# Low halves of six weight units per MLP pair: an accumulating transfer in place of a VectorE subtraction

## The chip, the cores and the metric

The kernel runs on one core of a Trainium2 chip. The metric is device time in microseconds, from the start to the end of one execution: the median over runs. The engines that matter here are TensorE (PE, the matmuls), VectorE (DVE), ScalarE (ACT), GpSimd (POOL), SyncE (SP, which only issues transfers) and the 16 DMA engines that move data for the queues of SP and POOL.

## The reference

Two layers of a decoder trunk on 256 tokens with a model width of 2048, all in float32. Each layer has a front part (a wide projection, sparse attention, a convolution branch, cross-attention, gates, an output projection) and then the part that the change touches, the MLP with a hidden width of 8192:

```
h2 = rms_norm(x, norm2_g[l])
x  = x + jnp.square(jax.nn.relu(h2 @ w_up[l])) @ w_down[l]
```

Weights are read from HBM once per layer. No weight stays on the chip.

## The kernel before, in words

**Split products.** PE is given float32 numbers in a rounded form. To keep the accuracy, each operand is written as a high part and a low part, and a product is three matmuls: high by high, high by low, low by high (function `product`, lines 877 to 879, and `unit`, lines 670 to 672). A weight tile is therefore prepared twice before PE may use it: ACT copies the raw tile into the rounded form (`hi`), and DVE subtracts that from the raw tile (`lo = raw - hi`).

**Units and rings.** SP loads weights in chunks of 1 MB (128 partitions by 4 by 512 numbers) into `raw`, which has four slots. One chunk is two *units*, and a unit is 128 by 1024 numbers of `raw`. The split parts lie in `hi` and `lo`, which have four places each, so unit number i of a pair uses place i % 4. ACT may write `hi` of a unit only when PE has finished the unit four before it (`unit_done`), DVE waits for ACT (`hi_ready`), and PE waits for DVE (`lo_ready`). SP loads a chunk into a slot again when the low parts of the units that lay there are made.

**Pairs.** In the MLP two column blocks of 512 are worked on together as a *pair* of 16 units (`seven_products`). For a quarter of the rows the pair saves one product in eight by multiplying sums of tiles. This is why units have different sizes on PE: units 0 and 1 are 6 matmuls each, units 2 and 3 are 12 each, units 4 and 5 only 3 each, units 6 to 11 are 12 each, then 24 matmuls with sums of weights (`w_sum`) follow, and units 12 to 15 are 12 each: 186 matmuls. The rows of the pair's eight chunks go through the slots a, b, c, d, b, d, a, c, where a to d are the four slots of `raw`. So the sixth chunk (units 10 and 11) is loaded into the slot where units 6 and 7 lay.

**Number of pairs.** A layer has four quarters (`qu`) of the hidden width, and a quarter has four pairs `j`: 0 and 1 for `w_up`, 2 and 3 for `w_down`. The last quarter of the first layer has only the first two and uses plain units for the rest. That makes 14 + 16 = 30 pairs. In pairs 1 and 2 of a quarter PE also turns the hidden numbers between its units (16 transposes, line 683), in pairs 0 and 3 it does not.

**Order.** Each engine's program is a list written out by hand. ACT does `hi` of each unit in order, with its other work between (`side_of_pair`, `hidden_of_pair`). DVE does `lo` of each unit in order, with the sums of weights (line 1767), their low parts (line 1771) and sums of results between. POOL has almost nothing to do in the MLP: one load of a gain vector (line 2106).

Of the kernel before, what the change touches and what calls it, by code (L numbers as in the profile page):

```python
# [15 lines left out]


# [1 line left out]

# [1 line left out]

# [3 lines left out]
F32 = mybir.dt.float32  # L25
F32R = mybir.dt.float32r
I32 = mybir.dt.int32
ALU = mybir.AluOpType
# [178 lines left out]
def paired(l, qu):  # L207

    return qu < FFN // D - 1 or l == LAYERS - 1


W_SUMS_AT = [6, 7, 8, 9]
# [63 lines left out]
def build(nc, x, mem, positions, norm1_g, w_in, q_norm_g, k_norm_g, mem_norm_g, w_mem_kv, mq_norm_g,  # L276
# [3 lines left out]
    with ctx:  # L280
# [148 lines left out]
        landed = [sem(f"landed{c}") for c in range(CHUNKS)]  # L429
        hi_ready = sem("hi_ready")  # L430
        lo_ready = sem("lo_ready")
        unit_done = sem("unit_done")
        acc_free = [sem(f"acc_free{i}") for i in range(2)]
        tp_full = sem("tp_full")
# [135 lines left out]
        @block.sync  # L570
        def _(sp):
            here = Place(["unit"])

            def load(c, source):

                sp.wait_ge(lo_ready, here.next("unit", 2))
                sp.sem_inc(waited, 1)
                c = here.ring[c]
                sp.dma_start(raw[:, c, :, 0:source.shape[-1]], source).then_inc(landed[c], 16)

            def load_pair(pair, source, c0):

                units = here.now("unit")
                slots = here.pair_slots()
                for k, (b, c) in enumerate(PAIR_CHUNKS):
                    here.next("unit", 2)
                    if k < 4:
                        sp.wait_ge(lo_ready, here.now("unit"))
                    elif k < 6:
                        sp.wait_ge(lo_ready, units + (12, 16)[k - 4])  # L590
                    else:
                        sp.wait_ge(w_summed, 4 * pair + 4)
                    sp.sem_inc(waited, 1)
                    sp.dma_start(raw[:, slots[k]], source[c, :, :, bass.ds(c0 + b * COL, COL)]).then_inc(landed[slots[k]], 16)

            for l in range(LAYERS):
                for q, (g, c) in enumerate(FRONT_CHUNKS):
                    view, c0, w = FRONT_SRC[g]
                    if l == 0 and q < CB:
                        cols = slice(q * COL, (q + 1) * COL)  # L600
                        if q == 1:
                            sp.wait_ge(first_gain[0], 16)
                            sp.sem_inc(waited, 1)
                        if q > 1:
                            sp.wait_ge(landed[q - 2], 16)
                            sp.sem_inc(waited, 1)
                        sp.dma_start(gain[:, cols], rows(norm1_g[0, cols])).then_inc(first_gain[q], 16)
                        sp.dma_start(x_tok[:, :, cols], x_rows[:, :, cols]).then_inc(x_in[q], 16)
                    if l == 0 and q == 0:
                        sp.wait_ge(lo_ready, here.next("unit", 2))  # L610
                        sp.sem_inc(waited, 1)
                        for half, there in enumerate((landed[0], first_rest)):
                            ks = slice(2 * half, 2 * half + 2)
                            sp.dma_start(raw[:, 0, ks, 0:w], view[l, c, :, ks, c0:c0 + w]).then_inc(there, 16)
                        continue
                    load(q % CHUNKS, view[l, c, :, :, c0:c0 + w])
                for cb in range(CB):
                    for i in range(3):
                        for c in range(CHUNKS):
                            load(c, v_in[l, c, :, :, bass.ds(GATE0 + i * D + cb * COL, COL)])  # L620
                    load(0, v_co[l, 0, :, :, bass.ds(cb * COL, COL)])
                    load(1, v_mo[l, 0, :, :, bass.ds(cb * COL, COL)])
                    load(2, v_ao[l, 0, :, :, bass.ds(cb * COL, COL)])
                    load(3, v_ao[l, 1, :, :, bass.ds(cb * COL, COL)])
                for b in range(CB):
                    for c in range(CHUNKS):
                        load(c, v_out[l, c, :, :, b * COL:(b + 1) * COL])
                for qu in range(FFN // D):
                    for j in range(2):
                        load_pair(pair_number(l, qu, j), v_up[l], qu * D + 2 * j * COL)  # L630
                    if paired(l, qu):
                        for j in range(2):
                            load_pair(pair_number(l, qu, 2 + j), v_down[l, qu], 2 * j * COL)
                        continue
                    for b in range(CB):
# [16 lines left out]
        def _(pe):  # L652
# [3 lines left out]
                pe.sem_inc(s, 1)  # L656
            pe.wait_ge(ready, 1)

            def unit(u, a_hi, a_lo, kts, w, pair, first, last):

                if first:

                    pe.wait_ge(acc_free[pair], here.next(f"acc{pair}"))
                pe.wait_ge(lo_ready, here.next("unit") + 8)
# [44 lines left out]
            def ikw_unit(s, u, first, last):  # L709

                if first:
                    pe.wait_ge(sc_free[0], here.next("sc0"))
                pe.wait_ge(lo_ready, here.next("unit") + 8)
# [175 lines left out]
            def seven_products(l, qu, j):  # L889
# [7 lines left out]
                for i, (b, u) in enumerate(PAIR_UNITS):  # L897
# [14 lines left out]
                    pe.wait_ge(lo_ready, here.next("unit") + 8)  # L912
# [108 lines left out]
        def _(act):  # L1021
# [254 lines left out]
            def split_of_pair(i, slots):  # L1276
# [6 lines left out]
                if b == 1 and u < SEVEN:  # L1283
                    act.activation(hi[:, i % 4, 1], raw[:, c, 2 * (i % 2) + 1], ACT.Copy).then_inc(hi_ready, 1)
                else:
                    act.activation(hi[:, i % 4], raw[:, c, 2 * (i % 2):2 * (i % 2) + 2], ACT.Copy).then_inc(hi_ready, 1)  # L1286

            def side_of_pair(i, pair, number):

# [80 lines left out]
        def _(dve):  # L1370
# [301 lines left out]
            def split_of_pair(i, slots):  # L1672

                b, u = PAIR_UNITS[i]
                c, rows_ = slots[i // 2], slice(2 * (i % 2), 2 * (i % 2) + 2)
                dve.wait_ge(hi_ready, here.next("unit"))
                if b == 1 and u < SEVEN:
                    ins = dve.tensor_tensor(lo[:, i % 4, 1], raw[:, c, 2 * (i % 2) + 1],
                                            hi[:, i % 4, 1].bitcast(F32), ALU.subtract)
# [241 lines left out]
        def _(pool):  # L1921
# [30 lines left out]
            def side(n, l):  # L1952
# [65 lines left out]
                if n == LN_APPLY:  # L2018
# [3 lines left out]
                    pool.tensor_tensor(y_tok[:, :, :], y_tok[:, :, :], over(ln_b[:, :], 1, T),  # L2022
                                       ALU.add).then_inc(ln_scaled, 1)

            def biases(l, c):

                alone()
# [21 lines left out]
            for l in range(LAYERS):  # L2049
# [49 lines left out]
                root(2)  # L2099
                here.next("fill", T * CB + 8 * (FFN // D) + T * (CB - 1))  # L2100

                if l < LAYERS - 1:
                    pool.wait_ge(scaled, here.next("scaled", T + CB))
                    pool.wait_ge(seven_free, pair_number(l, FFN // D - 1, 0))
                    alone()
                    pool.dma_start(gain[:, :], rows(norm1_g[l + 1])).then_inc(gain_in, 16)
                    here.next("scaled", CB - 1)
                here.layer_done()


# [21 lines left out]
```

## Time and profile before

| | |
|---|---|
| time | 2829.12 us, median of 2 runs (2828.1 and 2830.14) |
| profiled execution | span 2827.0 us; no other time of it is recorded, the runs lie 1.1 to 3.1 us above the span |
| PE | busy 2817.1 us, 12924 matmuls and transposes |
| DVE | busy 2063.3 us (73%) |
| ACT | busy 1558.7 us (55%) |
| POOL | busy 185.4 us (7%) |
| DMA | 557.76 MB; SP's queue takes 55.3% of the 16 engines' time, POOL's 3.5% |
| granted PE clock | 1.000 of full speed over the span |

A profile lists the instructions of one execution with their start and length. An engine's idle time is put down to what ended it. A busy PE is a pipelined one: matmuls of 390 ns start every 227 ns, so one lies over the next, and their rate is read from their starts.

### The profile page before, as it was taken

What the parts mean: (1) busy time and instruction counts of PE and PEld (TensorE: products, weight loads), DVE (VectorE), ACT (ScalarE), POOL (GpSimd) and SP (SyncE); (2) the same over time, 40 slices, a digit from 0 to 9 for tenths busy, and PEclk for the clock granted to TensorE, in tenths of its full rate; (3) what the DMA queues carried; (4) which work ended last, traced back from release to release, by engine and by line L of the source; (5) the groups of instructions that cost most, each with busy time, mean ns of one, the idle gap of its engine ahead of it and who ended that gap; (6) DMA issues with size and microseconds to landing.
All of it is one profiled execution on the core that took longest, in us unless ns stands there. A gap on an engine that the chain in (4) does not pass through costs nothing.

```text
span 2827.0 us, 32980 instructions
## 1 busy us (share of the span) xinstructions
PE 2817.1 (100%) x12924; PEld 2332.6 (83%) x12924; DVE 2063.3 (73%) x2247; ACT 1558.7 (55%) x2048; POOL 185.4 (7%) x205
## 2 busy tenths in 40 slices
PE   9999999999999999999999999999999999999999
PEld 7888888888888888888888888888888888888887
DVE  6688656556788888887656976555667887887887
ACT  6777644444554655555448776444455555455463
POOL 1124100000000000000002251000000000000000
PEclk9999999999999999999999999999999999999999
DMA  8655566755565565666566555667555655655645
GB/s 304 210 170 176 167 194 208 238 190 198 178 208 172 202 218 167 210 220 208 180 218 210 169 179 166 194 206 238 194 194 166 220 192 181 215 167 208 214 164 179
DMA packets 274795, 557.76 MB, mean 197 GB/s; under 512 B 13232, under 2 KB 13232, under 8 KB 272464
## 3 DMA queue, kind: packets, MB, share of 16 engines
q1 hardware_dynamic: 268896, 526.68, 55.3%
q0 software_dynamic: 5744, 28.97, 3.5%
q8 instruction: 102, 1.67, 0.2%
q14 instruction: 53, 0.43, 0.0%
HBM read 549.32 MB, written 6.29 MB: 197 GB/s over the span
## 4 chain that ended last, share of the span: by engine, by line
PE 99%; DMA 0%; ACT 0%; DVE 0%; issue 0%; SPq 0%; ACTq 0%; DVEq 0%
PE acc L670 17%; PE acc L672 17%; PE acc L671 16%; PE acc L879 13%; PE acc L878 13%; PE acc L877 13%; PE tp L683 3%; PE sc L879 1%; PE sc L878 1%; PE sc L877 1%; PE tp L878 1%; PE tp L877 1%; PE tp L879 1%; PE sc L733 0%; PE tp L763 0%; PE sc L730 0%
## 5 line engine op out<-in xcount | busy, mean ns | idle before, releaser
L1392 DVE TENSOR_TENSOR lo<-raw,hi 128x1024 fp32r<-128x1024 f32 (+1 forms) x528 | 648.5, 1232 | 491.2 <-ACT hi L1036 485.3
L1036 ACT ACTIVATE hi<-raw 128x1024 fp32r<-128x1024 f32 (+1 forms) x528 | 546.6, 1037 | 611.3 <-PE acc L672 588.4
L1286 ACT ACTIVATE hi<-raw 128x1024 fp32r<-128x1024 f32 x420 | 437.9, 1056 | 556.7 <-PE acc L879 359.7
L1681 DVE TENSOR_TENSOR lo<-raw,hi 128x1024 fp32r<-128x1024 f32 x420 | 509.7, 1221 | 107.1 <-ACT hi L1286 106.3
L670 PE MATMUL acc<-hi,hT 128*128 128x512 f32 x1280 | 509.4, 398 | 1.7 <-DVE lo L1392 1.7
L672 PE MATMUL acc<-hi,hT 128*128 128x512 f32 x1280 | 499.8, 390 | 0.0
L671 PE MATMUL acc<-lo,hT 128*128 128x512 f32 x1280 | 498.6, 390 | 0.0
L877 PE MATMUL acc<-hi,hT 128*128 128x512 f32 x800 | 312.2, 390 | 0.0
L879 PE MATMUL acc<-hi,hT 128*128 128x512 f32 x800 | 311.5, 389 | 0.0
L878 PE MATMUL acc<-lo,hT 128*128 128x512 f32 x800 | 311.4, 389 | 0.0
L672 PEld LDWEIGHTS acc<-hi,hT 128*128 128x128 f32 x1280 | 240.2, 188 | 51.7
L670 PEld LDWEIGHTS acc<-hi,hT 128*128 128x128 f32 x1280 | 240.5, 188 | 49.6 <-issue 2.1
L671 PEld LDWEIGHTS acc<-lo,hT 128*128 128x128 f32 x1280 | 240.8, 188 | 47.2
L877 PE MATMUL acc<-hi,bT_hi 128*128 128x512 f32 x700 | 273.0, 390 | 0.0
L879 PE MATMUL acc<-hi,bT_lo 128*128 128x512 f32 x700 | 272.5, 389 | 0.0
L878 PE MATMUL acc<-lo,bT_hi 128*128 128x512 f32 x700 | 272.4, 389 | 0.0
L670 PE MATMUL acc<-hi,bT_hi 128*128 128x512 f32 x512 | 203.7, 398 | 0.0
L672 PE MATMUL acc<-hi,bT_lo 128*128 128x512 f32 x512 | 199.9, 390 | 0.0
L671 PE MATMUL acc<-lo,bT_hi 128*128 128x512 f32 x512 | 199.5, 390 | 0.0
L877 PEld LDWEIGHTS acc<-hi,hT 128*128 128x128 f32 x800 | 150.2, 188 | 31.4
L879 PEld LDWEIGHTS acc<-hi,hT 128*128 128x128 f32 x800 | 150.2, 188 | 31.3
L878 PEld LDWEIGHTS acc<-lo,hT 128*128 128x128 f32 x800 | 150.2, 188 | 30.8
(331 smaller groups left out, 3951.0 us busy)
## 6 DMA issues: line engine op xcount, KB each, us to landing
raw<-in_w_in SPq DMA_DIRECT2D x159, 1024.0 KB, 5.0
raw<-in_w_up SPq DMA_DIRECT2D x128, 1024.0 KB, 6.0
raw<-in_w_down SPq DMA_DIRECT2D x128, 1024.0 KB, 5.5
raw<-in_w_out SPq DMA_DIRECT2D x32, 1024.0 KB, 5.2
raw<-in_w_mem_kv SPq DMA_DIRECT2D x16, 1024.0 KB, 5.1
raw<-in_w_attn_o SPq DMA_DIRECT2D x16, 1024.0 KB, 5.2
raw<-in_w_conv_o SPq DMA_DIRECT2D x8, 1024.0 KB, 5.1
raw<-in_w_mem_o SPq DMA_DIRECT2D x8, 1024.0 KB, 5.2
```

Source lines behind the costliest of these rows:

```text
L670: pe.matmul(o, a1, w1, start=first and dk == 0, stop=False)
L671: pe.matmul(o, a1, w2, start=False, stop=False)
L672: mm = pe.matmul(o, a2, w1, start=False, stop=last and dk == 1)
L683: mm = pe.transpose(tp[0:m, b, i, 0:k], tile, ident[0:k, 0:k])
L877: pe.matmul(o, a_hi, w_hi, start=first, stop=False)
L878: pe.matmul(o, a_hi, w_lo, start=False, stop=False)
L879: return pe.matmul(o, a_lo, w_hi, start=False, stop=last)
L1036: act.activation(hi[:, u % 4, :, 0:w], raw[:, c, 2 * (u % 2):2 * (u % 2) + 2, 0:w], ACT.Copy).then_inc(hi_ready, 1)
L1286: act.activation(hi[:, i % 4], raw[:, c, 2 * (i % 2):2 * (i % 2) + 2], ACT.Copy).then_inc(hi_ready, 1)
L1392: dve.tensor_tensor(lo[:, u % 4, :, 0:w], raw[:, here.ring[u // 2], 2 * (u % 2):2 * (u % 2) + 2, 0:w], hi[:, u % 4, :, 0:w].bitcast(F32), ...
L1681: ins = dve.tensor_tensor(lo[:, i % 4], raw[:, c, rows_], hi[:, i % 4].bitcast(F32), ALU.subtract)
```

## The change

In every pair, units 6, 7, 9, 12, 13 and 14 no longer get their low part from DVE. ACT writes the high part as before, waits for its own write, and then writes the negated high part into `lo`. POOL waits for that and issues a transfer from `raw` to `lo` that adds what it moves to what lies there, so `lo` ends as `raw - hi`. PE waits for that transfer (`lo_added`, one semaphore for each of the four places) where it waited for DVE. SP waits for it too before it overwrites the raw slot. All other units keep DVE's subtraction. The load of the gain vector stands on POOL between the transfers of the third and the fourth quarter. The diff, cut to its core:

```diff
+DMA_LOW = (6, 7, 9, 12, 13, 14)
+def by_dma(l, qu, j, i):
+    return (j < 2 or paired(l, qu)) and i in DMA_LOW
...
+            def units_split(n):
+                if n > 0:
+                    sp.wait_ge(lo_ready, 8 + LOWS[n])
+                    sp.sem_inc(waited, 1)
+                for r in {m % 4 for m in range(max(n - 8, 0), n) if BY_DMA[m]}:
+                    sp.wait_ge(lo_added[r], 16 * LOWS_MADE[r][n])
+                    sp.sem_inc(waited, 1)
...
                     if k < 4:
-                        sp.wait_ge(lo_ready, here.now("unit"))
+                        units_split(here.now("unit") - 8)
                     elif k < 6:
-                        sp.wait_ge(lo_ready, units + (12, 16)[k - 4])
+                        units_split(units + (4, 8)[k - 4])
...
+            def split_here():
+                n = here.next("unit")
+                if BY_DMA[n - 1]:
+                    pe.wait_ge(lo_added[(n - 1) % 4], 16 * LOWS_MADE[(n - 1) % 4][n])
+                else:
+                    pe.wait_ge(lo_ready, 8 + LOWS[n])
...
                     act.activation(hi[:, i % 4], raw[:, c, 2 * (i % 2):2 * (i % 2) + 2], ACT.Copy).then_inc(hi_ready, 1)
+                    if i in DMA_LOW:
+                        act.wait_ge(hi_ready, here.now("unit"))
+                        act.activation(lo[:, i % 4], hi[:, i % 4].bitcast(F32), ACT.Copy, scale=-1.0).then_inc(minus_hi, 1)
...
-                dve.wait_ge(hi_ready, here.next("unit"))
+                here.next("unit")
+                if i in DMA_LOW:
+                    return
+                dve.wait_ge(hi_ready, here.now("unit"))
...
+            def low_parts(pair):
+                slots = here.pair_slots()
+                for k, i in enumerate(DMA_LOW):
+                    pool.wait_ge(minus_hi, len(DMA_LOW) * pair + k + 1)
+                    alone()
+                    pool.dma_start(lo[:, i % 4].bitcast(F32), raw[:, slots[i // 2], 2 * (i % 2):2 * (i % 2) + 2],
+                                   accum_op=ALU.add).then_inc(lo_added[i % 4], 16)
```

ACT's list in the fourth pair of the program (first layer, first quarter, j = 3), units 4 to 10: the number behind `landed` is the slot of `raw`, and `hi_50`, `lo_51`, `raw_49` are the three buffers. Before:

```order
L1284 ACTIVATE hi_50<-raw_49 128x512 [waits unit_done,landed3]
L1284 ACTIVATE hi_50<-raw_49 128x512 [waits unit_done]
L1286 ACTIVATE hi_50<-raw_49 128x1024 [waits unit_done,landed1]
L1286 ACTIVATE hi_50<-raw_49 128x1024 [waits unit_done]
L1286 ACTIVATE hi_50<-raw_49 128x1024 [waits unit_done,landed0]
```

and in the changed kernel, where line 1286 is line 1324:

```order
L1322 ACTIVATE hi_50<-raw_49 128x512 [waits unit_done,landed3]
L1322 ACTIVATE hi_50<-raw_49 128x512 [waits unit_done]
L1324 ACTIVATE hi_50<-raw_49 128x1024 [waits unit_done,landed1]
L1327 ACTIVATE lo_51<-hi_50 128x1024 [waits hi_ready]
L1324 ACTIVATE hi_50<-raw_49 128x1024 [waits unit_done]
L1327 ACTIVATE lo_51<-hi_50 128x1024 [waits hi_ready]
L1324 ACTIVATE hi_50<-raw_49 128x1024 [waits unit_done,landed0]
```

The negated copies of units 6 and 7 stand directly behind their high parts, ahead of the high part of the next unit.

SP's list around the first pairs. Before (the last loads of the output projection, the first pair's first six and last two chunks, and the third pair's):

```order
L579 DMA raw_49<-in_w_out 128x4x512 [waits lo_ready] x16
L594 DMA raw_49<-in_w_up 128x4x512 [waits lo_ready] x6
L594 DMA raw_49<-in_w_up 128x4x512 [waits w_summed] x2
...
L594 DMA raw_49<-in_w_down 128x4x512 [waits lo_ready] x6
L594 DMA raw_49<-in_w_down 128x4x512 [waits w_summed] x2
```

and in the changed kernel the first pair's first five, its sixth, its last two, and the second pair's first two and third:

```order
L625 DMA raw_49<-in_w_up 128x4x512 [waits lo_ready] x5
L625 DMA raw_49<-in_w_up 128x4x512 [waits lo_ready,lo_added2,lo_added3]
L625 DMA raw_49<-in_w_up 128x4x512 [waits w_summed] x2
L625 DMA raw_49<-in_w_up 128x4x512 [waits lo_ready,lo_added1,lo_added2,lo_added3] x2
L625 DMA raw_49<-in_w_up 128x4x512 [waits lo_ready,lo_added0,lo_added1,lo_added2,lo_added3]
```

The sixth load (units 10 and 11) now waits for the transfers of units 6 and 7. SP's queue is in order, so the loads behind it wait as well.

## Rows read from the trace of the kernel before

**Rows 1.** The page: span, and busy time, share and instructions by engine.

```profile
span 2827.0 us, 32980 instructions
PE 2817.1 (100%) x12924; PEld 2332.6 (83%) x12924; DVE 2063.3 (73%) x2247; ACT 1558.7 (55%) x2048; POOL 185.4 (7%) x205
```

**Rows 2.** All waits of PE: waited for: us in total, times, longest us.

```profile
PE sc L981 <- POOL ident L2038: 3.0, 1, 3.0
PE acc L670 <- DVE lo L1392: 1.7, 1, 1.7
PE tp L683 <- DVE xg L1421: 0.9, 1, 0.9
PE tp L683 <- ACT y_tok L1043: 0.8, 2, 0.4
```

**Rows 3.** The page: splitting groups of the pairs, count, busy us, mean ns, idle.

```profile
L1286 ACT ACTIVATE hi<-raw 128x1024 fp32r<-128x1024 f32 x420 | 437.9, 1056 | 556.7 <-PE acc L879 359.7
L1681 DVE TENSOR_TENSOR lo<-raw,hi 128x1024 fp32r<-128x1024 f32 x420 | 509.7, 1221 | 107.1 <-ACT hi L1286 106.3
```

**Rows 4.** Timeline, fourth pair: PE, last matmul of units 2 and 3, first of unit 6.

```profile
861.96 0.39 PE L879 MATMUL acc<-hi,bT_lo 128*128 128x512 f32 x1
...
864.68 0.39 PE L879 MATMUL acc<-hi,bT_lo 128*128 128x512 f32 x1
...
866.27 0.39 PE L877 MATMUL acc<-hi,bT_hi 128*128 128x512 f32 x1
```

**Rows 5.** Timeline, the same pair: ACT, units 6, 7 to 9, 10, 11, 12 to 13.

```profile
862.45 1.06 ACT L1286 ACTIVATE hi<-raw 128x1024 fp32r<-128x1024 f32 x1 [2.15 <-PE acc L879]
865.11 2.96 ACT L1286 ACTIVATE hi<-raw 128x1024 fp32r<-128x1024 f32 x3 [1.60 <-PE acc L879]
872.80 1.06 ACT L1286 ACTIVATE hi<-raw 128x1024 fp32r<-128x1024 f32 x1 [4.73 <-DMA raw<-in_w_down]
...
875.66 2.94 ACT L1295 ACTIVATE w_sum_hi<-w_sum 128x1024 fp32r<-128x1024 f32 x3
878.51 1.99 ACT L1286 ACTIVATE hi<-raw 128x1024 fp32r<-128x1024 f32 x2
```

**Rows 6.** Timeline, the same pair: DVE, low parts of units 6 and 7.

```profile
863.54 1.23 DVE L1681 TENSOR_TENSOR lo<-raw,hi 128x1024 fp32r<-128x1024 f32 x1 [0.62 <-ACT hi L1286]
...
866.21 1.23 DVE L1681 TENSOR_TENSOR lo<-raw,hi 128x1024 fp32r<-128x1024 f32 x1 [0.30 <-ACT hi L1286]
```

**Rows 7.** Timeline, a pair with transposes (second of a quarter): ACT, unit 6.

```profile
947.91 1.06 ACT L1286 ACTIVATE hi<-raw 128x1024 fp32r<-128x1024 f32 x1
```

**Rows 8.** Timeline, the same pair: PE, first matmul of unit 6.

```profile
952.44 0.39 PE L877 MATMUL acc<-hi,hT 128*128 128x512 f32 x1
```

**Rows 9.** DMA issues of POOL one by one: count, KB, us from issue to landing.

```profile
ln_g<-in_conv_ln_g POOLq DMA_DIRECT2D x1, 256.0 KB, 3.3
x_park<-x_tok POOLq DMA_DIRECT2D x1, 1024.0 KB, 4.3
gain<-in_norm_g POOLq DMA_DIRECT2D x1, 1024.0 KB, 6.8
conv_bias<-in_conv_o_b POOLq DMA_DIRECT2D x1, 256.0 KB, 9.4
```

**Rows 10.** Windows of the fourth pair: us, busy by engine, PE clock, DMA share, GB/s.

```profile
863.00:866.00 3.00, 3.00 (x15) 2.50 (x14) 2.36 (x2) 1.40 (x2) 0.00 (x0) 1.00 0.37 141
866.00:869.00 3.00, 3.00 (x15) 2.45 (x15) 2.79 (x3) 2.07 (x3) 0.00 (x0) 1.00 0.22 17
878.00:881.00 3.00, 3.00 (x14) 2.46 (x14) 3.00 (x4) 2.50 (x3) 0.00 (x0) 1.00 1.05 395
```

**Rows 11.** The page: DMA queue of SP, packets, MB, share of 16 engines.

```profile
q1 hardware_dynamic: 268896, 526.68, 55.3%
```

**Rows 12.** Window of one whole pair's length, columns as in rows 10.

```profile
780.00:824.00 44.00, 44.00 (x203) 36.46 (x203) 36.85 (x39) 26.70 (x31) 0.00 (x0) 1.00 0.56 191
```

More of the change, by code:

```diff
@@ L18 @@
 from contextlib import ExitStack
+from itertools import accumulate
 import numpy as np
@@ L209, in paired @@
     return qu < FFN // D - 1 or l == LAYERS - 1
+DMA_LOW = (6, 7, 9, 12, 13, 14)
+PAIRS = LAST_PAIR + 1
+def by_dma(l, qu, j, i):
+    return (j < 2 or paired(l, qu)) and i in DMA_LOW
+MLP_UNITS = [(l, qu, j, i) for l in range(LAYERS) for qu in range(FFN // D) for j in range(4) for i in range(16)]
+MLP_FIRST = [(l + 1) * GROUPS * UNITS - 2 * UNITS * 4 * (FFN // D) for l in range(LAYERS)]
+BY_DMA = [False] * (LAYERS * GROUPS * UNITS)
+for l_, qu_, j_, i_ in MLP_UNITS:
+    BY_DMA[MLP_FIRST[l_] + 16 * (4 * qu_ + j_) + i_] = by_dma(l_, qu_, j_, i_)
+LOWS = [0, *accumulate(1 - by for by in BY_DMA)]
+LOWS_MADE = [[0] * (LAYERS * GROUPS * UNITS + 1) for r in range(4)]
+for r_ in range(4):
+    LOWS_MADE[r_] = [0, *accumulate(int(by and n % 4 == r_) for n, by in enumerate(BY_DMA))]
 W_SUMS_AT = [6, 7, 8, 9]
@@ L431, in build @@
         lo_ready = sem("lo_ready")
+        minus_hi = sem("minus_hi")
+        lo_added = [sem(f"lo_added{r}") for r in range(4)]
         unit_done = sem("unit_done")
@@ L572, in _ @@
             here = Place(["unit"])
+            def units_split(n):
[5 more added lines that the diff above has]
+                    sp.sem_inc(waited, 1)
             def load(c, source):
-                sp.wait_ge(lo_ready, here.next("unit", 2))
-                sp.sem_inc(waited, 1)
+                units_split(here.next("unit", 2) - 8)
                 c = here.ring[c]
@@ L587, in load_pair @@
                     if k < 4:
-                        sp.wait_ge(lo_ready, here.now("unit"))
+                        units_split(here.now("unit") - 8)
                     elif k < 6:
-                        sp.wait_ge(lo_ready, units + (12, 16)[k - 4])
+                        units_split(units + (4, 8)[k - 4])
                     else:
                         sp.wait_ge(w_summed, 4 * pair + 4)
-                    sp.sem_inc(waited, 1)
+                        sp.sem_inc(waited, 1)
                     sp.dma_start(raw[:, slots[k]], source[c, :, :, bass.ds(c0 + b * COL, COL)]).then_inc(landed[slots[k]], 16)
@@ L609, in _ @@
                     if l == 0 and q == 0:
-                        sp.wait_ge(lo_ready, here.next("unit", 2))
-                        sp.sem_inc(waited, 1)
+                        units_split(here.next("unit", 2) - 8)
                         for half, there in enumerate((landed[0], first_rest)):
@@ L663, in unit @@
                     pe.wait_ge(acc_free[pair], here.next(f"acc{pair}"))
-                pe.wait_ge(lo_ready, here.next("unit") + 8)
+                split_here()
                 for dk, kt in enumerate(kts):
@@ L712, in ikw_unit @@
                     pe.wait_ge(sc_free[0], here.next("sc0"))
-                pe.wait_ge(lo_ready, here.next("unit") + 8)
+                split_here()
                 for dk in range(2):
@@ L911, in seven_products @@
                         hidden_here(u, qu)
-                    pe.wait_ge(lo_ready, here.next("unit") + 8)
+                    split_here()
                     w = [(hi[:, i % 4, dk], lo[:, i % 4, dk]) for dk in range(2)]
@@ L2023, in side, with next_gain @@
                                        ALU.add).then_inc(ln_scaled, 1)
+            def next_gain(l):
+                pool.wait_ge(scaled, here.next("scaled", T + CB))
+                pool.wait_ge(seven_free, pair_number(l, FFN // D - 1, 0))
+                alone()
+                pool.dma_start(gain[:, :], rows(norm1_g[l + 1])).then_inc(gain_in, 16)
+                here.next("scaled", CB - 1)
+            def low_parts(pair):
+                slots = here.pair_slots()
+                for k, i in enumerate(DMA_LOW):
+                    pool.wait_ge(minus_hi, len(DMA_LOW) * pair + k + 1)
+                    alone()
+                    pool.dma_start(lo[:, i % 4].bitcast(F32), raw[:, slots[i // 2], 2 * (i % 2):2 * (i % 2) + 2],
+                                   accum_op=ALU.add).then_inc(lo_added[i % 4], 16)
             def biases(l, c):
@@ L2100, in _ @@
                 here.next("fill", T * CB + 8 * (FFN // D) + T * (CB - 1))
[L2102 to L2107, printed above, removed]
+                for qu in range(FFN // D):
+                    for j in range(4 if paired(l, qu) else 2):
+                        low_parts(pair_number(l, qu, j))
+                    if l < LAYERS - 1 and qu == FFN // D - 2:
+                        next_gain(l)
                 here.layer_done()
```

## The prediction

> **What bounds the kernel now.** I read the page's busy times first: PE is busy for 2817.1 of 2827.0 us [rows 1]. So all idle time of PE is 9.9 us, 0.35% of the span, and no change that leaves PE's matmuls alone can give back more. The view of waits says who causes it: PE waited 6.4 us in all, 5.6 of them in the first microseconds, and not once for a low part in the MLP [rows 2]. VectorE, which the change relieves, is busy for 73%, but nobody on PE's path waits for it. The granted clock is 1.00 in every window I looked at [rows 10, 12]. Last I read the timeline around units 6 and 7 of a pair, because there the distance between "place free" and "PE needs it" is shortest: only units 4 and 5, three matmuls each, lie between.
>
> **What goes away.** 6 x 30 = 180 subtractions at 1.22 us [rows 3]: 220 us of VectorE time. It was hidden under PE and is worth nothing on the path. At most the 9.9 us above could come back, and as the waits of PE lie outside the MLP, I count 0.
>
> **What is added on ScalarE.** 180 negated copies at 1.06 us (the rate of the other copies of that size [rows 3]): 190 us, 6.3 us a pair, where ScalarE is busy 26.7 of 44 us [rows 12]. Throughput is no question, but each stands in a chain, below.
>
> **Units 6 and 7: a new wait of PE.** In the fourth pair PE's last matmul of unit 2 ends at 861.96 + 0.39 = 862.35 and ScalarE starts the high part of unit 6 at 862.45 [rows 4, 5], a handover of 0.10 us. It ends at 863.51. VectorE began at 863.54, ended at 864.77 [rows 6], and PE needed unit 6 at 866.27 [rows 4]: 1.50 us were left over. In the new chain the negated copy runs from 863.54 to 864.60, POOL is told at about 864.70, the transfer takes T from issue to landing, and PE is told 0.10 later. PE is late by 864.80 + T - 866.27 = **T - 1.47 us**. In a pair with transposes the high part starts at 947.91 and PE needs unit 6 at 952.44 [rows 7, 8]: 947.91 + 1.06 + 0.03 + 1.06 + 0.20 + T - 952.44 = **T - 2.18 us**. There are 15 pairs of each kind (j = 0 and 3, j = 1 and 2), so the mean is T - 1.82.
>
> Nothing hides this. ScalarE cannot start sooner, because place 2 of `hi` is free only when unit 2 is done, and when PE stalls the next pair shifts with it, with the same distances. So 30 stalls add up.
>
> **How large is T?** No row shows an accumulating transfer. It moves 512 KB, but reads both the raw tile and the place it adds to, 1 MB in all. POOL's transfers took 3.3 us for 256 KB, 4.3 us for 1 MB that comes from the chip's own memory, and 6.8 us for 1 MB in the middle of the MLP [rows 9]. I take T = 4.3 us: it is the row nearest in source and in bytes read, and the DMA engines are little used in the moment when unit 6 needs them (0.37 and 0.22 of their time [rows 10]). The bounds are 3.3 (fewer bytes than this transfer writes) and 6.8 us. With 4.3 the stalls are 2.83 and 2.12 us, mean 2.48, times 30 = **74 us**. With 3.3 it is 44 us, with 6.8 it is 149 us.
>
> The Trainium skill, "DMA: Bandwidth & Descriptors", section "Anatomy of one DMA", gives 2.0 us and bytes by 436 GB/s for a transfer of this queue: 3.2 us for 512 KB. "Collectives: The Full Stack", section "The bandwidth ceiling", says that an add in a transfer costs no cycles but needs two source reads, which halves the rate: 2.0 + 2.4 = 4.4 us, an estimate from the two pages. By the first the stalls would be 41 us, by the second 77 us; both speak against this change, and no trace of before shows which is right.
>
> Unit 7 brings no second stall. Its high part runs 865.11 to 866.17 [rows 5], the negated copy to 867.26, so the transfer lands at 867.46 + T. PE wants it 12 matmuls or 2.72 us after it began unit 6 late: 866.27 + T - 1.47 + 2.72 = 867.52 + T. That is level, whatever T is.
>
> **Units 10 and 11 come later.** Their load waited for VectorE's low part of unit 7, done at 867.44 [rows 6]; the high part of unit 10 started at 872.80 [rows 5], 5.36 us later. Now the load waits for the transfer: high part at 867.46 + T + 5.36, low part ready 2.3 us later, at 875.1 + T. PE needs it 4 x 2.72 us behind unit 6, at 875.7 + T. This just fits, so I count 0, up to 1 us a pair if the transfer of unit 9 slows that load.
>
> **Units 12 to 14.** Between the start of high part 10 and that of high part 12 ScalarE has 878.51 - 872.80 = 5.7 us of work [rows 5]. So high part 12 starts at about 878.6 + T, its negated copy is done 2.2 us later, and with both handovers the low part lands at 880.9 + T plus its own time T'. PE needs unit 12 after six units and 24 matmuls, 21.8 us behind unit 6: at 886.6 + T. So PE waits if T' is over 5.7 us (by the same steps 6.0 with transposes). Here the loads behind the sixth run back to back and the DMA engines are full, 1.05 of their time [rows 10]. I therefore take the row from the busy middle of the MLP, 6.8 us [rows 9]: 1.1 and 0.8 us, mean 0.9, times 30 = **28 us**. Bounds: nothing with T' under 5.7, and 3.5 x 30 = 105 us with the 9.4 us of a transfer that queued behind another [rows 9].
>
> **Other queues.** SP waits for one to four semaphores more per load; it idles between loads. POOL's gain load stands behind 72 transfers of the first three quarters, and was waiting until then for the same pair anyway; 0. DMA engines: SP's 526.68 MB took 55.3% of 2827 us [rows 11], 2.97 us per MB. Six transfers of 0.52 MB written and 1.05 MB read add 9 to 19 us to a pair of 44 us at share 0.56 [rows 12]: 0.78 to 0.98. The DMA engines do not become the bound by bytes, but little is left.
>
> **Sum.** 74 + 28 = 102 us on the profiled execution, 2827.0 to 2929. The median of the runs is 2.1 us above the profiled span, so 2931 us, 3.6% slower.
>
> **Rivals.**
> 1. *The transfer is short* (T up to about 3.5 us and T' under 5.7). For it: SBUF on both sides, an idle DMA moment. 1 MB took 4.3 us, and at 2.97 us per MB the half of it would need some 1.5 us less, 2.8. Then the stall is 0.6 to 1.3 us, 29 us in all; with T = 3.5 it is 50. The time is 2858 to 2880, not slower by 2%. The point that decides: a mean stall of 1.9 us, T = 3.7. Chance 0.20.
> 2. *Transfers queue on each other and on the loads.* T = 6.8 and the full 105 us at units 12 to 14: 149 + 105, 3083 us. For it: the share near 0.98. Against it: units 6 and 7 fall into a pause of the loads. Something between my sum and this, 2990 to 3083: chance 0.13.
> 3. *PE's clock falls in the stalls.* No row shows it: the longest stall of PE in before was 3.0 us at the start [rows 2], and the clock stood at 1.00 in all windows here. Matmuls start every 227 ns at the upper level (from 864.68 to 866.27 there are seven steps, the last matmul of unit 3 and the six of units 4 and 5 [rows 4]); at the lower of the two levels, 1.2 instead of 2.4 GHz, a unit would take 2.72 us more. If one unit per pair ran so, that is 82 us on top, 3013 us. "TensorE: Matmul & The Clock Gate" of the Trainium skill (Part 1) says that idleness does this. Chance 0.12.
> 4. *VectorE's relief pays.* It would have to shorten PE's own work; the cap is 9.9 us, 2819 us. Faster by 2% is out of reach. Chance of that much 0.01, against.
>
> My forecast, stalls of 1.9 to 5 us a pair at full clock, has 0.54. Two per cent, about what a measurement of this kernel can tell from no change, is 57 us or 1.9 us a pair. So: faster 0.01, same 0.20, slower 0.79. The range reaches from T = 3.1 without the tail (2829 + 38) to a case between rivals 2 and 3 with the sum, 3050: 2867 to 3050. The forecast alone would be 2886 to 2980.
>
> **What would show it.** In the profile of the changed kernel: PE's waits in the MLP name the transfer into `lo`, 30 of them of 2 to 3 us at unit 6, and shorter ones at unit 12; POOL's transfers land 4 to 5 us after issue in the first third of a pair and 6 to 7 us in the last; the DMA share of a pair is 0.7 or more; VectorE's busy time is 220 us lower and ScalarE's 190 us higher. I am wrong if T is under 3.5 us, if PE's waits lie at units 10 to 15 rather than at 6, or if the clock is below 1.00.

## The result, and the profile after

The changed kernel takes 3015.28 us (median of two runs, 3012.7 and 3017.87), the kernel before 2829.12: 1.0659 times as long, with a 95% interval of 1.0639 to 1.0680. The forecast was 2931; the time lies inside the range of 2867 to 3050, 84 us above the forecast and outside the 2886 to 2980 of the forecast at full clock.

The profiled execution is 3010.9 us long, 183.9 us more than [rows 1]. The page of the changed kernel, span and busy times (as [rows 1]), queues ([rows 11]), two splitting groups and the POOL issues ([rows 3]), and the landing time of the new transfers:

```profile
span 3010.9 us, 33864 instructions
PE 2880.2 (96%) x12924; PEld 2359.0 (78%) x12924; DVE 1861.2 (62%) x2067; ACT 1743.1 (58%) x2228; POOL 337.8 (11%) x385
...
q1 hardware_dynamic: 268896, 526.68, 51.3%
q0 software_dynamic: 31664, 123.35, 20.4%
...
L1324 ACT ACTIVATE hi<-raw 128x1024 fp32r<-128x1024 f32 x420 | 440.7, 1053 | 555.9 <-PE acc L917 278.2
L1725 DVE TENSOR_TENSOR lo<-raw,hi 128x1024 fp32r<-128x1024 f32 x240 | 293.5, 1223 | 370.3 <-ACT hi L1324 370.2
...
L2083 POOL DMA_DIRECT2D lo<-raw x180 | 152.2, 846 | 1279.1 <-ACT lo L1327 1211.5
...
lo<-raw POOLq DMA_DIRECT2D x180, 512.0 KB, 5.4
```

VectorE lost its 180 subtractions (202 us) and ScalarE got 184 us. PE does the same 12924 matmuls, but is busy for 63.1 us more and idle for 120.8 us more. These two numbers are the 183.9 us. The waits of PE (us in total, times, longest) account for the idle part. The first two of these lines are new, the third stood in [rows 2] too:

```profile
PE acc L915 <- DMA lo<-raw: 109.0, 44, 4.4
PE acc L915 <- DVE lo L1725: 11.2, 10, 2.0
PE sc L1019 <- POOL ident L2099: 3.0, 1, 3.0
```

The longer busy time is mostly clock. The mean granted clock of the execution is 0.983, and 0.017 x 3010.9 = 51 us (an estimate; some 2 us of it fall into time in which PE stood still anyway). The fourth pair, which [rows 4 to 6] show of before, shows how it comes about. The timeline of ACT (start, duration, what ended the idle time before):

```profile
881.62 1.06 ACT L1324 ACTIVATE hi<-raw 128x1024 fp32r<-128x1024 f32 x1 [2.15 <-PE acc L917]
882.72 1.07 ACT L1327 ACTIVATE lo<-hi 128x1024 fp32r<-128x1024 f32 x1
...
897.96 1.06 ACT L1324 ACTIVATE hi<-raw 128x1024 fp32r<-128x1024 f32 x1 [8.55 <-DMA raw<-in_w_down]
```

and POOL's issue for unit 6:

```profile
884.36 0.85 POOL L2083 DMA_DIRECT2D lo<-raw  x1 [20.66 <-ACT lo L1327]
```

and PE, from the last matmul of unit 5 on:

```profile
885.22 0.39 PE L917 MATMUL acc<-hi,hidT_sum_lo 128*128 128x512 f32 x1
889.16 0.79 PE L915 MATMUL acc<-hi,bT_hi 128*128 128x512 f32 x1 [3.55 <-DMA lo<-raw]
889.75 0.63 PE L916 MATMUL acc<-lo,bT_hi 128*128 128x512 f32 x1
890.18 0.63 PE L917 MATMUL acc<-hi,bT_lo 128*128 128x512 f32 x1
890.60 0.63 PE L915 MATMUL acc<-hi,bT_hi 128*128 128x512 f32 x1
```

The negated copy ends at 883.79. POOL starts to issue 0.57 us later, the transfer lands 4.8 us after that, and at 889.16 PE goes on, after 3.55 us without work. Then its matmuls start every 427 ns instead of the 227 ns of [rows 4]: the lower of the two clock levels, 1.2 instead of 2.4 GHz. The windows over the same stretch (columns as in [rows 10]) say the same in the clock column:

```profile
884.00:888.00 4.00, 1.61 (x8) 0.99 (x6) 1.08 (x2) 3.68 (x4) 1.69 (x2) 1.00 0.61 115
888.00:892.00 4.00, 2.84 (x7) 2.27 (x8) 3.66 (x4) 1.38 (x2) 0.85 (x1) 0.55 0.96 182
892.00:896.00 4.00, 4.00 (x13) 3.12 (x12) 0.00 (x0) 0.00 (x0) 0.00 (x0) 0.60 1.02 236
896.00:900.00 4.00, 4.00 (x19) 3.31 (x18) 0.94 (x1) 2.04 (x3) 0.00 (x0) 1.00 1.05 398
```

The column to be careful with is PE's busy time: at 892 to 896 it is 4.00 of 4.00 us, and yet only 13 matmuls ran, where 896 to 900 holds 19. The last two columns show the other surprise: the DMA engines are at 0.96 of their time while they move 182 GB/s; with loads alone a full share is some 400.

Each stall of PE can be put to the unit that it stands before, by its time and by the transfer that lands in that moment. Against the terms of the prediction:

| where the 183.9 us are | predicted | measured |
|---|---|---|
| unit 6, 30 stalls: 3.2 to 3.4 us in most pairs without transposes, 2.4 to 2.6 in most others | 74 | 91.2 |
| units 9 and 10: 7 stalls on a transfer, 10 on VectorE | 0 | 24.7 |
| units 12 to 14, 7 stalls | 28 | 4.3 |
| clock below 1.00 | 0 | 51 |
| PE busy longer, clock aside (63.1 - 51; the last section has a reading) | 0 | 12 |
| other idle time of PE | 0 | 0.6 |

### The profile page after: what moved, and what is told of

It is laid out like the page before. It is cut to its first block, busy times and chain, and to the rows that moved or that the text cites. A ratio compares the mean times of both kernels' runs of the same rounds, so it can differ in the third digit from the quotient of the medians.

```text
span 3010.9 us, 33864 instructions
## 1 busy us (share of the span) xinstructions
PE 2880.2 (96%) x12924; PEld 2359.0 (78%) x12924; DVE 1861.2 (62%) x2067; ACT 1743.1 (58%) x2228; POOL 337.8 (11%) x385
## 4 chain that ended last, share of the span: by engine, by line
PE 81%; DMA 11%; ACT 5%; issue 1%; DVE 1%; POOL 0%; SPq 0%; POOLq 0%; ACTq 0%; DVEq 0%
PE acc L708 16%; PE acc L710 16%; PE acc L709 15%; PE acc L915 9%; PE acc L916 9%; PE acc L917 9%; DMA lo<-raw 7%; PE tp L721 2%; ACT hi L1324 2%; DMA raw<-in_w_up 2%; DMA raw<-in_w_down 2%; ACT lo L1327 1%; ACT w_sum_hi L1336 1%; PE sc L917 1%; PE sc L916 1%
## 5 line engine op out<-in xcount | busy, mean ns | idle before, releaser
L1725 DVE TENSOR_TENSOR lo<-raw,hi 128x1024 fp32r<-128x1024 f32 x240 | 293.5, 1223 | 370.3 <-ACT hi L1324 370.2
L708 PE MATMUL acc<-hi,hT 128*128 128x512 f32 x1280 | 509.4, 398 | 2.4 <-DVE lo L1433 2.4
L710 PE MATMUL acc<-hi,hT 128*128 128x512 f32 x1280 | 499.8, 390 | 0.0
L709 PE MATMUL acc<-lo,hT 128*128 128x512 f32 x1280 | 498.6, 390 | 0.0
L915 PE MATMUL acc<-hi,hT 128*128 128x512 f32 x800 | 327.0, 409 | 70.0 <-DMA lo<-raw 64.0
L915 PE MATMUL acc<-hi,bT_hi 128*128 128x512 f32 x700 | 284.8, 407 | 50.4 <-DMA lo<-raw 45.1
L916 PE MATMUL acc<-lo,hT 128*128 128x512 f32 x800 | 322.3, 403 | 0.0
L917 PE MATMUL acc<-hi,hT 128*128 128x512 f32 x800 | 321.3, 402 | 0.0
L2083 POOL DMA_DIRECT2D lo<-raw x180 | 152.2, 846 | 1279.1 <-ACT lo L1327 1211.5
L916 PE MATMUL acc<-lo,bT_hi 128*128 128x512 f32 x700 | 280.7, 401 | 0.0
L710 PEld LDWEIGHTS acc<-hi,hT 128*128 128x128 f32 x1280 | 240.2, 188 | 51.6
L917 PE MATMUL acc<-hi,bT_lo 128*128 128x512 f32 x700 | 280.4, 401 | 0.0
L708 PEld LDWEIGHTS acc<-hi,hT 128*128 128x128 f32 x1280 | 240.5, 188 | 50.6 <-issue 2.6
L709 PEld LDWEIGHTS acc<-lo,hT 128*128 128x128 f32 x1280 | 240.7, 188 | 47.2
L915 PEld LDWEIGHTS acc<-hi,hT 128*128 128x128 f32 x800 | 156.2, 195 | 117.2 <-DMA lo<-raw 75.8
L915 PEld LDWEIGHTS acc<-hi,bT_hi 128*128 128x128 f32 x700 | 136.2, 195 | 90.9 <-DMA lo<-raw 33.2
L708 PE MATMUL acc<-hi,bT_hi 128*128 128x512 f32 x512 | 203.7, 398 | 0.0
L710 PE MATMUL acc<-hi,bT_lo 128*128 128x512 f32 x512 | 199.9, 390 | 0.0
L709 PE MATMUL acc<-lo,bT_hi 128*128 128x512 f32 x512 | 199.5, 390 | 0.0
```

What stands on the lines that cost most here:

```text
L915: pe.matmul(o, a_hi, w_hi, start=first, stop=False)
L916: pe.matmul(o, a_hi, w_lo, start=False, stop=False)
L917: return pe.matmul(o, a_lo, w_hi, start=False, stop=last)
L1725: ins = dve.tensor_tensor(lo[:, i % 4], raw[:, c, rows_], hi[:, i % 4].bitcast(F32), ALU.subtract)
L2083: pool.dma_start(lo[:, i % 4].bitcast(F32), raw[:, slots[i // 2], 2 * (i % 2):2 * (i % 2) + 2], accum_op=ALU.add).then_inc(lo_added[i % 4] ...
```

## The experiments

My theory was that of the prediction: a transfer costs where the distance from "high part written" to "PE needs it" is shorter than the chain, which is at unit 6 above all. The rival: the transfers and the loads slow each other, wherever they meet. Two questions stood beside that: what makes one transfer so long, and whether the lost clock comes from the stalls or from the transfers as such.

### No low parts at all: what VectorE's relief is worth

The six units get no low part from anyone; PE and the loads wait for the high part only.

```diff
-                    pe.wait_ge(lo_added[(n - 1) % 4], 16 * LOWS_MADE[(n - 1) % 4][n])
+                    pe.wait_ge(hi_ready, n)
```

> The low parts of the six units are not made at all, neither by VectorE nor by a transfer: PE uses what lies in the place, and waits for the high part alone. It shows what taking the six subtractions off VectorE is worth when nothing replaces them. If VectorE is off PE's path, as the waits of before say: 2824 to 2829 us, no more than the 9.9 us in which PE idled. If VectorE's load slows PE in a way that the waits do not show: under 2800 us.

Measured: 2828.94 us, 1.0001 [0.9991, 1.0010]. Taking 180 subtractions out of VectorE without putting anything in their place gives nothing back, within 0.1%. So nothing that replaces them can win time through VectorE's relief.

### Which units cost

Only the list of units changes, as here; the others are the same line with (7, 9, 12, 13, 14), (9, 12, 13, 14), (12, 13, 14) and (12,):

```diff
-DMA_LOW = (6, 7, 9, 12, 13, 14)
+DMA_LOW = (6, 7)
```

> Only units 6 and 7 by a transfer. Slack theory: the 30 stalls at unit 6 (91 us in the changed kernel) and the time that the lower clock takes behind them (some 60 us) stay, the stalls at units 9 and 12 to 14 (some 15 us) go: 2975 to 2995 us. Rival, load on the DMA engines: one third of the transfers, so about one third of 186 us: 2890 us.

> Unit 6 is back on VectorE, 7, 9, 12, 13, 14 stay with the transfer. Slack theory: place 3 is free when unit 3 is done, and PE needs it three units later; the chain for unit 7 is as long as that for unit 6, so the stall moves from unit 6 to unit 7 and keeps its size, about 3.4 us in pairs 0 and 3 and 2.4 us in pairs 1 and 2: 2990 to 3015 us. If the stall were due to two transfers in a row or to unit 6 alone, it goes: 2860 to 2900 us.

> Units 6 and 7 are back on VectorE, 9, 12, 13 and 14 stay with the transfer. Slack theory: no stall at 6 or 7; at unit 9 the high part ends at 868.1 in the fourth pair of before, the chain at about 874.7 with a landing of 5.0, PE needs it at 874.4: 0.3 us; in pairs with transposes ScalarE is 1 to 2 us later: about 2 us. 15 x 0.3 + 15 x 2 = 35 us and a little by the clock: 2850 to 2885 us. Rival, load on the DMA engines: four of six transfers, some 2950 us.

> Only units 12, 13 and 14 of each pair get their low part by a transfer; 6, 7 and 9 are back on VectorE. Slack theory (a transfer costs PE what the chain of high part, negated copy, hand-over and transfer takes beyond the time between 'place free' and 'PE needs it'): units 12 to 14 have about 13 us from place free to use, the chain takes 8 to 10 us, so no stall at units 6 to 10, full clock, and 2829 to 2840 us. Rival, the transfers cost by loading the DMA engines and queueing with the weight loads: the DMA engines are at a share of 1.0 just where these three run, so three of six transfers keep about half of the 186 us: some 2920 us.

> Unit 12 alone by transfer. With units 12 to 14 its transfer took 8.3 us (median) to land and TensorE waited 2.1 us in each pair. If it is the two transfers issued 2 and 4 us behind it that slow it, it lands in 5.0 to 6.5 us now, no wait is left, and the time is 2829 to 2840. Rival: the loads of weights slow it by themselves: 7.5 us or more, waits of 1 to 2 us in each pair, 2860 to 2900.

Measured (the cost of the clock is one minus the mean granted clock, times the span):

| units by transfer | us | ratio to before | PE waits on a transfer | clock |
|---|---|---|---|---|
| 6, 7, 9, 12, 13, 14 | 3015.3 | 1.0659 [1.0639, 1.0680] | 109.0 in 44 | 51 |
| 7, 9, 12, 13, 14 | 3020.0 | 1.0674 [1.0652, 1.0695] | 106.3 in 44 | 54 |
| 6, 7 | 2971.9 | 1.0506 [1.0485, 1.0527] | 90.1 in 31 | 50 |
| 9, 12, 13, 14 | 2886.2 | 1.0201 [1.0184, 1.0218] | 38.9 in 52 | 0 |
| 12, 13, 14 | 2916.2 | 1.0301 [1.0284, 1.0318] | 63.4 in 30 | 32 |
| 12 | 2920.6 | 1.0325 [1.0304, 1.0346] | 60.3 in 29 | 26 |

(Waits and clock are those of the profiled execution. With 12, 13 and 14 it was 2926.8 us long, the longest of that kernel's runs, 2909.1 to 2926.8.)

Units 6 and 7 behaved as the distances said: the second to the fourth row of the table lie only 5 us above, 3 below and 1 above their expected ranges. Taking unit 6 out saves nothing, because unit 7 then stalls PE in its place (84.8 us in 30 stalls). What fell are my expectations for the late units. I had expected hardly a wait with 12 to 14 alone, and the number came out at the rival's 2920. The run with unit 12 alone settles why: there too the rival was right, and its 2860 to 2900 us were even 20 us short, because the waits were 2.1 us each and the clock fell. One transfer alone, with no other behind it, still lands late. From its page, the transfers' count, size and landing time:

```profile
lo<-raw POOLq DMA_DIRECT2D x30, 512.0 KB, 8.1
```

One pair of it in windows of 2 us:

```profile
892.00:894.00 2.00, 2.00 (x11) 1.65 (x10) 1.17 (x2) 2.00 (x4) 0.85 (x1) 1.00 1.06 387
894.00:896.00 2.00, 2.00 (x11) 1.65 (x10) 2.00 (x3) 1.43 (x2) 0.00 (x0) 1.00 1.03 368
896.00:898.00 2.00, 2.00 (x11) 1.65 (x10) 0.10 (x1) 0.00 (x0) 0.00 (x0) 1.00 1.08 310
898.00:900.00 2.00, 1.51 (x7) 0.93 (x5) 0.37 (x1) 0.00 (x0) 0.00 (x0) 1.00 0.84 170
```

POOL's timeline there:

```profile
892.67 0.85 POOL L2083 DMA_DIRECT2D lo<-raw  x1 [45.10 <-ACT lo L1327]
```

and PE's, first matmul of unit 12:

```profile
900.73 0.50 PE L915 MATMUL acc<-hi,bT_hi 128*128 128x512 f32 x1 [1.22 <-DMA lo<-raw]
```

At issue the loads keep the DMA engines full (1.06), and for the first 4 us nearly all bytes are theirs. The transfer lands 8.0 us after issue, and PE starts. It does not take its siblings to slow it.

In the changed kernel the same transfer meets fewer loads. What the queues moved in the 4 us behind its issue in the fourth pair (packets, MB, share of 16 engines), first with unit 12 alone, from 892.67:

```profile
q1 hardware_dynamic: 734, 1.47, 102.2%
```

and then in the changed kernel, from 906.38:

```profile
q0 software_dynamic: 126, 0.52, 65.2%
q1 hardware_dynamic: 323, 0.63, 42.8%
```

With unit 12 alone POOL's queue (q0) moved nothing in these 4 us. In the changed kernel the loads (q1) moved 0.63 MB beside it, and the transfer landed in 4.8 us. SP's timeline says why fewer loads are left there: the sixth, seventh and eighth load of that pair (start of the first, us to the end of the third issue), before, with units 12, 13 and 14 alone, and in the changed kernel:

```profile
867.52 6.59 SPq L594 DMA_DIRECT2D raw<-in_w_down  x3
879.20 6.60 SPq L625 DMA_DIRECT2D raw<-in_w_down  x3
891.85 2.54 SPq L625 DMA_DIRECT2D raw<-in_w_down  x3
```

The seventh and the eighth wait for VectorE's sums of weights (`w_summed`). In the changed kernel the sixth is held until unit 7's transfer has landed, the sums are made by then, and the other two go out with it.

The table's other lesson is that rows do not add up. Unit 12 alone costs more than units 12, 13 and 14 together with 9. A stall gives everything behind it a lead: the loads, ScalarE and the transfers go on while PE stands. With unit 9 in the list, PE waits some 0.7 us there and reaches unit 10 1.1 us later (counted from its start of unit 8, means of 30 pairs); unit 12's transfer goes out 0.4 us sooner. Together that is the 1.5 us by which the wait at unit 12 fell, from 60.3 to 16.0 us, 2.0 to 0.5 a pair. The 0.4 us are probably not the lead: VectorE no longer makes unit 9's low part and ends its sums of weights 1.1 us sooner. No run separates the two. And waits of 1.6 us at most, 52 of them, left the granted clock at 1.00, where 31 waits of mostly 2.4 to 3.4 us cost 50 us of clock.

### What makes the transfer long

First without the add (the low part is then the raw weight), then with the add for the first half of the unit only (the second half stays the negated high part):

```diff
-                    pool.dma_start(lo[:, i % 4].bitcast(F32), raw[:, slots[i // 2], 2 * (i % 2):2 * (i % 2) + 2],
-                                   accum_op=ALU.add).then_inc(lo_added[i % 4], 16)
+                    pool.dma_start(lo[:, i % 4].bitcast(F32), raw[:, slots[i // 2], 2 * (i % 2):2 * (i % 2) + 2]
+                                   ).then_inc(lo_added[i % 4], 16)
```

```diff
+                    pool.dma_start(lo[:, i % 4, 0].bitcast(F32), raw[:, slots[i // 2], 2 * (i % 2)],
+                                   accum_op=ALU.add).then_inc(lo_added[i % 4], 16)
```

> The six transfers move the raw weights without adding (so the low part is wrong: it is the raw weight); all waits stay. It prices the addition. If the addition costs by its second read: the DMA time of one transfer falls from 2.9 us of all 16 engines to about 1.5, its landing in the quiet moment of unit 6 from 4.5 to about 3.1 us, the stalls at unit 6 from 3.3 and 2.6 to about 1.9 and 1.2 us, 46 us in all, and with less or no fall of the clock 2880 to 2910 us. If a transfer of POOL's queue costs the same with and without the addition: 3015 us.

> The six transfers add only the first half of the unit (128 by 512), the second half keeps the negated high part (a wrong low part). It splits the landing of 4.5 us into a fixed part and one by bytes. If the bytes set it (2.9 us of DMA time for the whole): 3.1 us, the stalls at unit 6 about 1.9 and 1.2 us, 2880 to 2910 us. If the fixed part sets it: landing over 4 us, 2990 to 3015 us.

Measured: 2966.59 us, 1.0485 [1.0464, 1.0506], and 2983.79 us, 1.0546 [1.0525, 1.0567]. Neither range was hit. The transfers themselves did what the first theory said. Landed one by one, the transfer of unit 6 takes 4.5 us (median of 30) in the changed kernel, 3.3 with half of it added and 2.8 as a plain copy. The time of the DMA engines comes from the queue's share on each page. The kernel without low parts gives the base of that queue:

```profile
q0 software_dynamic: 5744, 28.97, 3.4%
```

The page of the kernel with plain copies:

```profile
span 2963.9 us, 33864 instructions
...
q0 software_dynamic: 31664, 123.35, 11.5%
```

Plain: (0.115 x 2963.9 - 0.034 x 2826.4) / 180 = 1.36 us of all 16 engines for one transfer. With the add: (0.204 x 3010.9 - 96) / 180 = 2.88 us. The same bytes by the page's count take 2.1 times as long. "Collectives: The Full Stack" of the Trainium skill, section "The bandwidth ceiling", says of the add in a ReduceScatter that it needs two source reads, which halves the rate. The factor of 2.1 here agrees with that; that the second read is the reason here too is not shown.

But the gain did not reach the end. The waits of PE with plain copies:

```profile
PE acc L915 <- DMA lo<-raw: 97.1, 57, 4.1
```

At unit 6 the stalls fell from 91.2 to 38.9 us, the amount that 4.5 to 2.8 us gives (30 x 1.7 = 51). At unit 9 they rose from 13.5 us in 7 stalls to 54.7 us in 25, and unit 9's transfer took 7.0 us (median) to land instead of 5.6, although it now takes half of the DMA engines' time. SP's next loads, which wait for units 6 and 7, are released sooner and run into unit 9's transfer: in the fourth pair the first of them goes out 0.09 us before it (881.06 and 881.15), in the changed kernel 1.86 us behind it (891.85 and 889.99). And with shorter stalls PE gives less lead. With half of the unit added it is the same: 46.6 us at unit 6 and 52.1 at unit 9. A faster transfer moved the wait by three units.

### Is it the stall that lowers the clock, and does a stall give a lead?

Matmuls into an unused accumulator stand ahead of PE's wait at unit 6, as long as the stalls there: 15 in pairs j = 0 and 3, 11 in j = 1 and 2, but none in the first pair of a layer.

```diff
+                    if i == 6 and not first_of_layer:
+                        for _ in range(15 if j in (0, 3) else 11):
+                            pe.matmul(sc[:, 1], hT_hi[:, 0, 0:P], hT_hi[:, 0:2], start=True, stop=True)
```

First with all six units:

> The changed kernel, and PE does matmuls of 128 by 512 that nobody reads (15 in pairs 0 and 3 of a quarter, 11 in pairs 1 and 2, none in the first pair of a layer) between unit 5 and its wait for unit 6: 366 matmuls of 227 ns, 83 us, about as long as the stalls. If the lower clock is a consequence of PE standing idle at unit 6: the stalls turn into work, the clock stays at 1.00, and the 60 us go: about 2955 us although PE does more. If the clock falls for another reason, or the lost time is not the clock: 3010 to 3020 us, as the changed kernel. If the stalls were not where I put them, the matmuls come on top: 3095 us.

Measured: 3028.52 us, 1.0704 [1.0688, 1.0720]. The 2955 us did not come. The clock rose from 0.983 to 0.992, and the stalls at unit 6 fell to 0.7 us or less, except in the two pairs that have no fill. But at unit 9 the seven long ones grew from 0.9 to 2.6 us to 2.4 to 3.9, and waits on VectorE's low parts grew from 11.2 us in 10 to 23.4 in 19. The lead would explain it: those seven lie in pairs j = 1, where PE in the changed kernel loses some 2.6 us at unit 6 and 1.7 us by the clock behind it, 4.3 us together; the fill holds it for 11 x 0.24 = 2.6 us, 1.7 us less, and six of the seven grew by 1.2 to 1.6 us. Two things were mixed here, so I took them apart, with the same fill in two smaller lists.

> Units 6 and 7 by transfer, and 15 idle-filling matmuls (11 in pairs 1 and 2 of a chunk) that write an unused accumulator ahead of TensorE's wait at unit 6. Their 360 x 0.227 us = 82 us are in the time, and take the place of the 90 us of waits seen with units 6 and 7 alone. If the clock falls because TensorE stood idle, the 53 us of slower matmuls go with the waits: 2829 + 82 + some 5 to 10 of waits left = 2915 to 2925, with a granted clock of 1.0, so faster than units 6 and 7 alone (2972) in spite of 360 more matmuls. Rival: the clock falls because of the transfers or the work around them: the clock stays at .983 and the time is 2960 to 2980.

Measured: 2939.29 us, 1.0392 [1.0375, 1.0410]. That is 14 us above the expected range, and 33 us *less* than units 6 and 7 without the fill (2971.9), though PE has 360 matmuls more to do. The waits of PE on the transfer, filled:

```profile
PE acc L915 <- DMA lo<-raw: 11.0, 10, 4.4
```

and the fill's own group of instructions (busy, mean ns, idle):

```profile
L952 PE MATMUL sc<-hT 128*128 128x512 f32 x360 | 86.3, 389 | 0.0
```

The windows around unit 6 of the fourth pair, with units 6 and 7 alone:

```profile
882.00:884.00 2.00, 0.00 (x0) 0.00 (x0) 0.62 (x1) 2.00 (x3) 0.84 (x1) 1.00 1.04 199
884.00:886.00 2.00, 1.11 (x3) 0.89 (x4) 2.00 (x3) 0.29 (x1) 0.00 (x0) 0.83 1.04 195
886.00:888.00 2.00, 2.00 (x6) 1.61 (x5) 2.00 (x3) 0.00 (x0) 0.00 (x0) 0.50 0.53 98
```

and filled:

```profile
880.00:882.00 2.00, 2.00 (x11) 1.65 (x10) 0.08 (x1) 2.00 (x3) 0.48 (x1) 1.00 0.99 188
882.00:884.00 2.00, 2.00 (x10) 1.42 (x8) 2.00 (x2) 0.84 (x1) 0.36 (x1) 1.00 0.93 174
884.00:886.00 2.00, 2.00 (x10) 1.67 (x9) 2.00 (x3) 0.00 (x0) 0.00 (x0) 1.00 0.86 162
```

The same two transfers run in both (DMA share about 1 with under 200 GB/s), but where PE has work, its clock stays at 1.00; the mean went from 0.983 to 0.998. So the clock falls because PE stands idle, not because of the transfers. Of the 14 us over the range, 4 are fill that took 86 instead of 82 us, and some 4 to 6 the clock that is still lost, most of it behind the 4.4 us stall of a pair without fill; the rest was not traced.

> Units 12, 13 and 14 by transfer, and the same 360 matmuls (82 us) ahead of unit 6, where nothing waits in this kernel. If a hold of TensorE at unit 6 gives the loads, ScalarE and the transfers of units 12 to 14 a lead of the same 2.5 to 3.4 us, the 63 us of waits at unit 12 (1.2 to 4.4 in each pair) fall under 15 us and the clock returns to 1.0: 2829 + 82 + 5 to 15 = 2915 to 2926, hardly more than units 12 to 14 alone (2916) although 82 us of work came in. Rival: the loads are held as long as TensorE is, so that the lead does not grow and the costs add: 2916 + 82 = 2998.

Measured: 2924.53 us, 1.0338 [1.0323, 1.0354], as expected from the lead. The waits at unit 12:

```profile
PE acc L915 <- DMA lo<-raw: 11.9, 11, 2.1
```

They were 63.4 us in 30. The fill adds 86 us of PE time at unit 6 and the kernel is only 8 us longer than without it. The transfers still land in 7.9, 8.5 and 8.9 us (medians of units 12, 13, 14), hardly sooner than without the fill (8.3, 8.8, 9.3). PE simply comes later. So holding PE at unit 6 pays for the units behind it.

## Why the prediction was right and wrong, point by point

- **Bound and VectorE's relief: right.** 0 was counted, and the kernel without low parts shows 0 within 0.1%.
- **Unit 6: right in mechanism, 17 us short.** That the stall is T less a constant stands. T was 4.5 (median) where I took 4.3 [rows 9], which is 6 us over 30 pairs. The handover was mis-sized: PE to ScalarE was read from [rows 4, 5] as 0.10 us, but ScalarE to POOL is 0.57 (883.79 to 884.36, above), and with hardly any behind the landing the two handovers cost 0.57 instead of 0.20; 0.37 x 30 = 11 us. With both, T - 1.10 and T - 1.81 give 3.4 and 2.7 us, where 3.2 to 3.4 and 2.4 to 2.6 were measured.
- **Unit 7: right.** It brings no second stall; and with unit 6 gone it has the whole one.
- **Units 10 and 11 "just fits, so I count 0": wrong, and unit 9 had no term of its own.** 24.7 us came in at units 9 and 10. In seven of the eight second pairs (j = 1) unit 9's transfer lands 8.4 to 9.6 us after its issue: SP's loads that waited for units 6 and 7 go out in the same moment (SP at 791.75, POOL at 791.77 us in the first of them). These 13.5 us the prediction did not price. Ten times PE waits for VectorE's low part of unit 10, 11.2 us in all; in those pairs its load took 6.7 to 8.9 us to land beside unit 9's transfer (5.3 us in the fourth pair of before). I had put this as "up to 1 us a pair if the transfer of unit 9 slows that load", which is the mechanism, and 0.4 us a pair is what it cost.
- **Units 12 to 14, 28 us: wrong in T'.** The distance was right: in the changed kernel PE needs unit 12 5.7 us (median) after POOL's issue, and with only units 12 to 14 by transfer it is 8.3 less the 2.1 us of wait, 6.2; the sum had 5.7 and 6.0. The step that failed is T' = 6.8 us, taken because the loads fill the DMA engines there. With units 12 to 14 alone they do: T' was 8.3 us, and the waits were 63 us, not 28. In the changed kernel the transfers landed in 5.6, 5.95 and 6.6 us, and 4.3 us were left. The sum moved the loads behind the sixth back by T, like the sixth itself. But they do not wait for the transfers; they go out with the sixth (above) and are mostly through when POOL issues. So "74 + 28" could not be added: the transfers of the first term take the loads out of the way of the second.
- **Clock, counted 0: wrong.** Rival 3, "PE's clock falls in the stalls", came with 51 us instead of its 82, because only part of a unit ran slowly (1.7 us lost a pair, not 2.72). I gave it 0.12, because the only long idle time in before was at the start and said nothing. The Trainium skill's "TensorE: Matmul & The Clock Gate" (Part 1), which says that idleness does this, is borne out by the filled kernel: mean clock 0.998 instead of 0.983.
- **The total.** Rival 3's 3013 us lies nearest to 3015, but by a different sum: 102 + 82, where 120.8 + 63.1 was measured. That the time lies inside the range is in part luck: the range reached so far up only for a case between rivals 2 and 3, and the 24 us too many for units 12 to 14 made good the 25 us that were missing for units 9 and 10. One of the prediction's own signs of being wrong came true, "if the clock is below 1.00"; the other two, a short T and the waits at units 10 to 15, did not.

## What to carry to other kernels

Price a wait of the bound engine twice: the wait, and the clock behind it. Here the second was nearly half as much again (51 against 120 us), and the 52 waits of up to 1.6 us in the kernel with units 9, 12, 13 and 14 had none of it. Stalls of one pipeline are not added: work out the first one, give its length as a lead to whatever does not wait for the same thing, and only then look whether the next still waits; a repair of the first stall can wake the next, as it did at unit 9 here. And work taken off an engine that nobody waits for is worth nothing, whatever its busy share says.

## What the runs showed of the hardware that was not expected

- A transfer that adds, from SBUF to SBUF, 512 KB: 4.5 us to land with the loads paused, 8.1 with the load queue full (medians of 30), 9.6 at most in the changed kernel. It takes 2.88 us of all 16 engines, against 1.36 for the copy. GpSimd's issue takes longer too: 846 ns instead of 528, the mean on the page with plain copies.
- A wait costs PE a little more than its length even at full clock. With units 9, 12, 13 and 14 the clock is 1.00, but PE is busy for 2834.3 us, 17.2 more than before, in 52 waits: 0.33 us each. Two parts of it can be read. The last matmul before a wait counts as busy for its 0.39 us, where otherwise the next would start after 0.227: 0.16 us. And the timeline of PE in that kernel shows 0.34 us from the first matmul behind a wait to the second, instead of 0.227: 0.11 us.

```profile
835.66 0.50 PE L915 MATMUL acc<-hi,bT_hi 128*128 128x512 f32 x1 [0.25 <-DMA lo<-raw]
836.00 0.39 PE L916 MATMUL acc<-lo,bT_hi 128*128 128x512 f32 x1
836.23 0.39 PE L917 MATMUL acc<-hi,bT_lo 128*128 128x512 f32 x1
```

  The 54 waits of the changed kernel at 0.33 us would be 18 us (an estimate), enough for the 12 us of its busy time that the clock does not explain.

- Stalls of the same length do not always end the same way: behind the 3.29 us stall at 937.75 in the changed kernel the clock stayed at 1.00, and so it did behind four more of 2.5 to 3.3 us, out of 30 at unit 6. What tells them apart stays open.
